# A ninth extra block of experts computed ahead in a hybrid decoder layer with product-key experts

## What is computed

```python
q = (hf @ w_query).reshape(n, PEER_HEADS, 2, PEER_HALF)          # 8 heads
scores = jnp.einsum('nhpd,hpkd->nhpk', q, sub_keys)
s_top, i_top = lax.top_k(scores, 16)
...                                                              # 16 best of the 256 sums
gates = jax.nn.softmax(best_s, axis=-1)
u = jnp.take(expert_u, idx_blk, axis=0)
act = jax.nn.gelu(jnp.einsum('thkd,td->thk', u, h_blk))
vv = jnp.take(expert_v, idx_blk, axis=0)
y = jnp.einsum('thk,thkd->td', g_blk * act, vv)
```

## Time and profile before

| | |
|---|---|
| median of 3 runs | 2925.73 us (2925.23 to 2926.56) |
| the profiled execution | 2921.54 us, span 2919.8 us |
| TensorE matmuls busy | 2817.2 us (96%) |
| VectorE busy | 2417.2 us (83%) |
| ScalarE (ACT) busy | 1118.8 us (38%) |
| GpSimd (POOL) busy | 1228.6 us (42%) |
| DMA | 770.97 MB, mean 264 GB/s |
| granted TensorE clock, mean | 0.993 |

### The profile page before, as it was taken

One profiled execution on the slowest core, in us unless ns is written; L12 is line 12 of the kernel. 1 busy time (PEld: TensorE's weight loads), 2 busy tenths in 40 slices (PEclk: granted clock), 3 DMA queues, 4 the chain that ended last, 5 costly groups with the idle time before them and its releaser, 6 DMA issues.

```text
span 2919.8 us, 48126 instructions
## 1 busy us (share of the span) xinstructions
PE 2817.2 (96%) x16232; PEld 2500.5 (86%) x16232; DVE 2417.2 (83%) x4565; ACT 1118.8 (38%) x2211; POOL 1228.6 (42%) x989
## 2 busy tenths in 40 slices
PE   5999999999999999999999999999999999999997
PEld 4888888788788889988888898899888888888896
DVE  6345666675689999979999989889898999999898
ACT  7222544523355556643333333233332333232233
POOL 0001000010178830026666556555556555655564
PEclk9999999999999999999999999999999999999999
DMA  7427444244311129899999999999999999999999
GB/s 281 158 91 235 118 116 116 98 144 146 140 44 43 46 97 289 269 343 371 367 354 372 370 340 355 335 333 358 352 359 355 347 367 358 371 361 354 356 365 285
DMA packets 334588, 770.97 MB, mean 264 GB/s; under 512 B 21968, under 2 KB 160752, under 8 KB 328312
## 3 DMA queue, kind: packets, MB, share of 16 engines
q0 software_dynamic: 117296, 423.15, 38.7%
q1 hardware_dynamic: 209448, 342.22, 34.6%
q10 hardware_dynamic: 7712, 3.93, 0.4%
HBM read 692.62 MB, written 76.60 MB: 263 GB/s over the span
## 4 chain that ended last, share of the span: by engine, by line
PE 37%; DVE 17%; DMA 7%; issue 7%; DVEq 3%; POOL 2%; ACT 1%; POOLq 0%; ACTq 0%; SPq 0%
PE psum L2578 17%; PE psum L2571 16%; DMA ex_v_row<-in_expert_v,ex_row 5%; DVE ex_u_row L2827 3%; DVE acc L2839 2%; PE psum L203 2%; DVE sc_hg L2241 1%; DVEq L2240 1%; DVE sc_hi L2235 1%; DMA w_dram<-sc_w 1%; DMA ex_u_row<-in_expert_u,ex_row 1%; DVE sc_hj L2232 1%; DVE rt_rest L2002 1%; DVE ex_v_lo L2822 1%; POOL ex_v_row L2529 1%
## 5 line engine op out<-in xcount | busy, mean ns | idle before, releaser
L2529 POOL DMA_INDIRECT ex_u_row<-in_expert_u,ex_row x384 | 415.4, 1082 | 702.6 <-DVE ex_dot L2827 397.1
L2529 POOL DMA_INDIRECT ex_v_row<-in_expert_v,ex_row x384 | 536.1, 1396 | 163.5 <-issue 109.2
L2839 DVE SCALAR_TENSOR_TENSOR acc<-ex_v_row,ex_coef,acc 128x1024 f32<-128x1024 f32 x381 | 489.3, 1284 | 52.6 <-DMA ex_v_row<-in_expert_v,ex_row 52.3
L2827 DVE CUSTOM_DVE_ANT_0 ex_u_row<-ex_u_row,h_rows 128x1024 f32<-128x1024 f32 x384 | 466.9, 1216 | 7.6 <-DMA ex_u_row<-in_expert_u,ex_row 7.4
L2578 PE MATMUL psum<-ex_v_hi,ex_c_lo 128*128 128x512 f32 x1260 | 342.5, 394 | 13.7 <-DVE ex_v_lo L2822 13.5
L2578 PE MATMUL psum<-ex_v_lo,ex_c_hi 128*128 128x512 f32 x1260 | 338.7, 391 | 0.0
L2578 PE MATMUL psum<-ex_v_hi,ex_c_hi 128*128 128x512 f32 x1260 | 337.4, 390 | 0.0
L2571 PE MATMUL psum<-h_hi,h_lo 128*128 128x320 f32 x1664 | 279.6, 310 | 11.8 <-DVE acc L2901 9.0
L2578 PEld LDWEIGHTS psum<-ex_v_hi,ex_c_lo 128*128 128x128 f32 x1260 | 234.4, 189 | 63.5 <-issue 17.2
L2578 PEld LDWEIGHTS psum<-ex_v_lo,ex_c_hi 128*128 128x128 f32 x1260 | 237.7, 189 | 50.4
L2578 PEld LDWEIGHTS psum<-ex_v_hi,ex_c_hi 128*128 128x128 f32 x1260 | 237.2, 188 | 49.8
(11 more groups left out here) (369 smaller groups left out, 5309.4 us busy)
## 6 DMA issues: line engine op xcount, KB each, us to landing
ex_vn<-in_expert_v SPq DMA_DIRECT2D x64, 1024.0 KB, 7.5
ex_un<-in_expert_u_t SPq DMA_DIRECT2D x40, 1024.0 KB, 8.5
ex_w<-w_dram SPq DMA_DIRECT2D x64, 640.0 KB, 10.3
w_dram<-sc_w SPq DMA_DIRECT2D x9, 4096.0 KB, 15.0
gm_wm<-in_w_mod_rest SPq DMA_DIRECT2D x28, 512.0 KB, 6.0
ex_un<-in_expert_u_t SPq DMA_DIRECT2D x24, 512.0 KB, 7.8
pj_raw<-in_w_in SPq DMA_DIRECT2D x11, 1024.0 KB, 6.5
pr_wm<-in_w_mod_first SPq DMA_DIRECT2D x8, 1024.0 KB, 14.5
```

The costliest lines, as they stand in the source:

```text
L2529: nc.gpsimd.indirect_dma_start(to[:], None, all_rows, bass.IndirectOffsetOnAxis(row[s][:, col:col + 1], 0)).then_inc(done, 16)
L2827: nc.vector.tensor_tensor_reduce(out=u_row[k % 3][:], in0=u_row[k % 3][:], in1=h_rows[:, k % 3, :], scale=1.0, scalar=0.0, op0=ALU.mult, o ...
L2839: nc.vector.scalar_tensor_tensor(out=to, in0=v_row[k % 3][:], scalar=coef[:, k:k + 1], in1=to, op0=ALU.mult, op1=ALU.add).then_inc(row_use ...
```

## The change

One constant of `Ahead` goes from 8 to 9:

```diff
@@ -1580,7 +1580,7 @@
     FIRST, IN_HEADS, IN_TAIL = 2, 6, 6
     HEADS = IN_HEADS + IN_TAIL
     EVERY = NKEYS // 8
-    EXTRA = 8
+    EXTRA = 9
     BLOCKS = EVERY + EXTRA
 
     def __init__(self, nc, core, t, expert_u, expert_u_t, h):
```

## The result

The changed kernel takes 2929.19 us (median of 20 runs) where the kernel before takes 2925.01 (20 runs). The ratio is 1.0015, with a 95% interval of 1.0009 to 1.0021: **4.4 us more**, between 2.6 and 6.1. It is slower, by less than the 0.2% that I had called no change, and the forecast was +3.8.

The account below looks back on a forecast made before the run. No single engine was taken as the bound everywhere; TensorE limits periods with one ready block. A 9.2 us cost at the hand-over less 5.4 gained in the loop gave +3.8, so 2929.5 us on the median, range 2923 to 2936.

Parts of the forecast that it names:

- The new wait: Scatter's end: ACT's first loop split waits for every half ahead, until 1256.4; VectorE 7.6 us late, TensorE hole 4.8 us.
- The clock: Loop's first half on TensorE: a granted clock near 0.5 behind the new hole loses 1.5 us.
- Rival (b): Hand-over: half clock lasts through group 38's products, group 39's start 13.0 us late, sum +7.6; chance 0.09.
- Filled holes as a gain: Groups 36 and 37 on TensorE: new work fills holes, group 37's products run at full clock, 0.75 us won.
- All shifts together behind group 39: Loop's entry: stores, loads and gathers hang on group 39's eviction, so its whole delay of 9.2 us carries on.
- relief of up to 1 us: Loop's entry: tile 8's store and u block 1's load are out of the way earlier, so 1 us could return.
- The loop: One 104.84 us period becomes an eighth late one of about 99.48: gain 5.4 us, bounds 2.3 and 7.05.
- (a): Loop: the added late period meets the row wait, over 101.5 us, gaining only 2.3; sum +6.9; chance 0.17.
- (c): Loop's entry: the stall is absorbed because saturated transfers set the entry; sum -5.4 to -7.05 us; chance 0.08.
- (d): Loop: TensorE sets the late periods, so the full 7.05 us is gained; sum +2.1; chance 0.12.

Follow-up runs that it names:

- dve_later: The changed kernel with VectorE's two splits moved one group back, behind group 38's one-hots; 1.0012 against the kernel before, +3.5 us.
- filler28: The changed kernel with 28 matmuls that nobody reads in TensorE's hole before the loop's first half; 1.0007 against the kernel before, +2.0 us.
- before_filled17: The kernel before with 17 matmuls that nobody reads in TensorE's 2.70 us hole behind group 36's products; 1.0001, no change.
- scatter_alone: The changed kernel's scatter with the thirteenth block, but the loop keeps LATE = 7 and computes it again; 1.0039 against the kernel before, +11.4 us.
- loop_alone: The kernel before with only the loop's LATE = 6, reading another block's results for the missing one (wrong values); 0.9979, -6.1 us.
- reorder13: The changed kernel with the loop's first halves after group 39 and the last tile's stores ahead of block 1's split; 1.0012 against the kernel before, +3.5 us.

## Why the prediction was right

- **The new wait.** Right in place and size. Less the shift, in the order of the prediction (predicted, measured): group 36's products 1245.45, 1245.43; job 12's first half ended 1250.9, 1250.85; its second 1256.3, 1256.26; ACT's split 1256.4, 1256.5; VectorE's splits 1257.6, 1257.6; group 38's one-hots 1259.95, 1259.9; the loop's first half started 1261.1, 1260.9. The number came from replaying the queues with durations of the trace and asking at each wait which of its conditions is met last. That VectorE is 7.6 us late was right (7.54 of waiting) and, as `dve_later` shows, not what counts.
- **The clock.** Right in kind, small by 0.9 us: I gave the half 5.2 us, from products that lost 1.5 behind holes of 2.70 and 4.19 us. It took 6.12, all but the last of it at a low clock, and `filler28` prices the loss at 2.3. It started 0.2 earlier than I had it, so the cost came to 9.9 at group 39, where the sum has 9.2: of the cost, this is the mis-sized term. Rival (b), the low clock lasting through the next products, did not come: those ran 1.82 us at 1.00.
- **Filled holes as a gain.** I counted 0.75 us won at group 37's products. Those did get shorter, but `before_filled17` shows that the low clock there had cost the kernel before nothing, since VectorE reached group 38 at the same time. The 0.75 was inside the replay and was no error in the sum, but against the kernel before nothing was won.
- **All shifts together behind group 39.** Nearly: 9.9 late at group 39, 9.1 at the first load of ready results, 8.9 in `scatter_alone`. The prediction had named an entry less late than group 39 as a sign of being wrong; the 0.8 us are the relief of up to 1 us that it left in its range, and TensorE's hole ahead of step 2's halves fell from 2.84 to 1.74 us. From the first load to index 6 the lateness grew again to 10.7, and the tail gave 1.4 back. In the other kernels that stretch gives or takes between -2.4 and +3.4 us, and 6.3 and 7.8 in the two reordered ones. Its cause, and that of the tail's 1.4, stay open.
- **The loop.** 5.4 predicted. The windows of indices 6 and 7 gave 6.2 and `loop_alone` took 6.1 off the time, but the sum prices indices 6 to 14, and over these the trace gained 4.65. These nine windows take 897.9 to 899.9 us in the eight traces with two ready blocks from index 6, and 901.7 to 905.7 in the five that have them from index 7: means of 898.9 and 903.5, 4.6 apart. So this term was some 0.8 too large by the traces; by the time of `loop_alone` it could as well have been too small. The mean of late windows was the right row (99.48 and 99.52), and the full 7.05 didn't come. The rule of the Trainium skill (Perfetto Trace Analysis, "Identifying the Most-Contended Engine") doesn't speak for it either: it says which engine to optimize first and gives no amount, and it has TensorE's headroom judged by its share of peak FLOP/s or by the busy time of its weight loads, not of its matmuls. The weight loads were busy for 613.12 us of the 696.33, VectorE for 644.83, so by this measure VectorE was the busier one.
- **How near the number is.** By the trace both terms missed the same way, the cost by 0.7 and the gain by 0.8: 9.9 - 4.65 is +5.3. The entry, the periods up to index 6 and the tail changed that by -0.8, +1.6 and -1.4 to the 4.7 at the end of the span, and the times say +4.4 (2.6 to 6.1). That the forecast of +3.8 lies 0.6 from the measured median is in part luck; a difference of that size can't be told from noise here.
- **Rivals.** (a) needed a new late period over 101.5 us; it took 98.28. (c), an absorbed stall, is refuted by `scatter_alone` at +11.4. (d), the full gain of 7.05, is further than the forecast's 5.4 from both the 4.65 of the trace and the 6.1 of `loop_alone`; its sum of +2.1 lies outside the measured interval.

## What to carry to other kernels

A wait on a counter that covers *everything* before it ("all halves ahead") costs nothing while the last of them is early, and takes effect when work is added at the end; look for it before adding, and ask which part the next step really needs, as waiting for the one place took 7 of the 10 us at group 39 off here, and 4.4 us off the kernel. Adding work to fill an engine's holes also moves the last point that others wait for, so replay each engine's queue past the place, including the DMA issues in it. And price a lowered clock only where that engine is the later one: the same kind of hole cost 2.3 us in one kernel and nothing in the other.

## What was new about the hardware

The time for which ACT is held by issuing the same two stores (3.8 MB) ran from 5.3 us in the changed kernel to 14.4 in `reorder13`; what sets it was not tried. A gathered row was late at the same step in all thirteen kernels, by 3.6 to 5.1 us, whatever the time around it.
